# The output stage of a streaming encoder layer: seven half-contraction products for a pair of token tiles in place of eight

## The reference: what is computed

```python
def layer(x, ...):
    proj = jnp.einsum('bld,de->ble', rmsnorm(x, norm_pre), w_in)
    ...                       # three branches: y_gla, y_pool, y_gdn
    merged = gts[:, :, 0] * y_gla + gts[:, :, 1] * y_pool + gts[:, :, 2] * y_gdn
    y = merged.astype(x.dtype) @ w_out          # (2112 x 1024) @ (1024 x 1024)
    x = x + rmsnorm(y, norm_post)
```

## Time and profile before

| | us |
|---|---|
| median of 3 runs | 2485.74 |
| lowest and highest run | 2482.61, 2487.33 |
| profiled execution, first to last instruction | 2480.0 |
| output stage in it: first matmul to last | 2285.5 to 2470.8 |
| end of the last VectorE instruction | 2476.1 |
| PE busy over the span | 2421.5 (98%) |
| VectorE, ScalarE, GpSimd busy over the span | 1104.4, 684.1, 847.1 |

### The profile page before, as it was taken

The page is one execution under the profiler, slowest core; times in us unless marked ns, Lnnn a source line. Parts: engine busy times, 40 slices in busy tenths (PEclk is TensorE's granted clock), DMA queues, the critical chain, the costliest instruction groups (busy, mean ns, idle before and its releaser), DMA issues. The chain is left out here.

```text
span 2480.0 us, 38129 instructions
## 1 busy us (share of the span) xinstructions
PE 2421.5 (98%) x14815; PEld 2263.5 (91%) x14815; DVE 1104.4 (45%) x1867; ACT 684.1 (28%) x1379; POOL 847.1 (34%) x760
## 2 busy tenths in 40 slices
PE   7999999999999999999999999999999979999998
PEld 7989999999999999998999999899998979999886
DVE  6620111223466664006666665666656453224333
ACT  6211111110155531112233223332233243213221
POOL 1212212212111121215556655566555423334222
PEclk9999999999999999999999999999999989999999
DMA  5213512101111122232332343723433174544443
GB/s 168 75 70 113 210 60 78 44 35 49 55 53 52 54 94 79 89 112 78 106 87 80 98 126 89 225 80 99 127 87 86 53 286 167 202 171 133 152 148 101
DMA packets 200892, 264.92 MB, mean 107 GB/s; under 512 B 16224, under 2 KB 176240, under 8 KB 195312
## 3 DMA queue, kind: packets, MB, share of 16 engines
q1 hardware_dynamic: 200816, 263.86, 33.0%
HBM read 164.54 MB, written 99.29 MB: 106 GB/s over the span
## 5 line engine op out<-in xcount | busy, mean ns | idle before, releaser
L393 PE MATMUL dense<-h,w_hi 128*128 128x416 f32 (+1 forms) x1640 | 590.4, 360 | 0.0
L394 PE MATMUL dense<-h,w_hi 128*128 128x416 f32 (+1 forms) x1640 | 582.0, 355 | 0.0
L395 PE MATMUL dense<-h,w_lo 128*128 128x416 f32 (+1 forms) x1640 | 581.4, 354 | 0.0
L188 POOL TENSOR_TENSOR w_hi<-w_raw,zero 128x1024 fp32r<-128x1024 f32 x77 | 148.8, 1933 | 1090.1 <-PE dense L395 795.2
L1443 PE MATMUL gate_bank<-h,w_hi 128*128 128x352 f32 x1632 | 421.7, 340 | 0.2 <-SPq L1301 0.2
L393 PEld LDWEIGHTS dense<-h,w_hi 128*128 128x128 f32 x1640 | 310.1, 189 | 13.5 <-issue 5.7
L394 PEld LDWEIGHTS dense<-h,w_hi 128*128 128x128 f32 x1640 | 308.7, 188 | 11.3 <-issue 4.5
L395 PEld LDWEIGHTS dense<-h,w_lo 128*128 128x128 f32 x1640 | 309.1, 188 | 7.0
L1443 PEld LDWEIGHTS gate_bank<-h,w_hi 128*128 128x128 f32 x1632 | 272.9, 189 | 9.2 <-issue 1.2
L1443 PE MATMUL gate_bank<-h,w_lo 128*128 128x352 f32 x816 | 264.1, 324 | 0.0
L2447 PE MATMUL y<-o_hi,wo_hi 128*128 128x352 f32 x576 | 189.3, 329 | 12.3 <-PEq L107 6.6
(11 more groups left out here) (240 smaller groups left out, 3975.5 us busy)
## 6 DMA issues: line engine op xcount, KB each, us to landing
w_raw<-in_w_in SPq DMA_DIRECT2D x77, 512.0 KB, 5.9
rows_then_inputs<-scratch_feat SPq DMA_DIRECT2D x16, 1856.0 KB, 9.4
scratch_feat<-row_y SPq DMA_DIRECT2D x28, 1056.0 KB, 4.9
gate<-scratch_gates SPq DMA_DIRECT2D x11, 2112.0 KB, 8.6
scratch_gates<-gate_row SPq DMA_DIRECT2D x102, 176.0 KB, 1.8
o_raw<-scratch_branch_out SPq DMA_DIRECT2D x6, 2112.0 KB, 13.5
scratch_h_second<-h SPq DMA_DIRECT2D x2, 4224.0 KB, 19.4
h<-scratch_h_second SPq DMA_DIRECT2D x6, 1408.0 KB, 7.8
```

The source lines that it names most:

```text
L188: nc.gpsimd.tensor_tensor(self.hi[:, p], raw, zeros, ALU.add).then_inc(self.high_ready, 1)
L393: nc.tensor.matmul(out, w_hi[:, p, k], hi.tile(k, t), start=(k == 0), stop=False)
L394: nc.tensor.matmul(out, w_hi[:, p, k], lo.tile(k, t), start=False, stop=False)
L395: mm = nc.tensor.matmul(out, w_lo[:, p, k], hi.tile(k, t), start=False, stop=(k == KD - 1))
```

## The change

The weight and a pair of two token tiles are taken as 2x2 blocks: tokens by contraction halves (A11, A12, A21, A22: 128 tokens by 512) and contraction halves by output halves (B11, B12, B21, B22: 512 by 512). In place of the eight block products the output stage forms seven, of sums and differences of the blocks (the names in the code: `P1` to `P7`; weight sides `B11, T2, T1, T3, B21, B22, T4`), and combines them.

- **PE**: a pair is 7 products of 12 matmuls (4 contraction blocks, 3 parts) in the order P1, P6, P5, P7, P2, P3, P4, in four PSUM banks: P1 and P2 in bank 0, P6 in bank 1, P5 and P3 in bank 2, P7 and P4 in bank 3. The later product of a bank waits until the earlier has been taken out. The code is written out, without a loop.
- **GpSimd**: for each pair the four sums `s1`, `a21` (in place), `s2`, `s4` of 128x512 (`sums`), ahead of the additions of the input row of the pair before (`result`), and one weight difference `T3` of 128x2048.
- **VectorE**: the lower part of each of the seven left operands (`a_low`, 128x512 each), five combinations of a bank with what is there (`taken`), the refined root, and the scaling, which now reads `y_row` in SBUF; for the weight seven lower parts of 128x2048 (`b_low`) and three differences `T1`, `T2`, `T4` of the same size.
- **ScalarE**: seven upper parts of 128x512 a pair and two copies out of bank 0, the squares from `y_row`; seven upper weight parts of 128x2048.
- **SyncE**: one load of `m_raw` for a pair (1 MB) into one of two buffers; the second buffer lies where the first pair's sums and the branch stage's weights are, so that its load waits for all seven weight parts (`b_split`) and six lower parts of pair 0.
- **The sample tile** keeps four half products, of 12 matmuls each, with A of 64 tokens.

The core of the diff:

```diff
+PRODUCTS = 7
+P1, P6, P5, P7, P2, P3, P4 = range(PRODUCTS)
+B_ORDER = (B11, T1, T2, T3, B21, B22, T4)
+PAIRS = CHUNKS // 2
...
+        bank_of = {P1: 0, P2: 0, P6: 1, P5: 2, P3: 2, P7: 3, P4: 3}
+        banks = [y_tok[:, 0], y_tok[:, 1], y[:, 0, 0], y[:, 0, 1]]
+        squares = y[:, 1, 1:3].rearrange("p a b -> p (a b)")
...
@@ sync
+                sp.wait_ge(b_split, PRODUCTS)
                 sp.dma_start(gain[:, :], d["norm_post"].to_broadcast([P, DM])).then_inc(gain_landed, 16)
-                sp.wait_ge(y_ready, LAST * KD + 1)
-                load_x(0, 0)
-                load_x(1, 1)
+                sp.wait_ge(a_split, P4)
+                load_m(1)
+                load_x(0)
+                load_x(1)
+                for i in range(PAIRS):
+                    if i + 2 <= PAIRS:
+                        sp.wait_ge(a_split, PRODUCTS * (i + 1))
+                        load_m(i + 2, 2 * P if i + 2 < PAIRS else NS_)
+                    for t in (2 * i, 2 * i + 1):
+                        store(t)
...
@@ tensor
-                    for half in range(2):
-                        cols = slice(half * 512, half * 512 + 512)
-                        out = tokens_bank(p)[0:n, cols]
-                        for k in range(KD):
+                def product(i, j):
+                    pe.wait_ge(a_split, PRODUCTS * i + j + 1)
+                    if i == 0:
+                        pe.wait_ge(b_split, split_by(j))
...
+                    elif j == P2:
+                        pe.wait_ge(act_taken, 2 * i + 1)
+                    elif j == P3:
+                        pe.wait_ge(dve_taken, 5 * i + 2)
+                    elif j == P4:
+                        pe.wait_ge(dve_taken, 5 * i + 3)
+                    later = j in (P2, P3, P4)
+                    blocks(banks[bank_of[j]], j, j, P, not later, True).then_inc(product_done, 1)
...
@@ vector
+                for i in range(1, PAIRS - 1):
+                    a_low(i + 1, P1)
+                    taken(i, P6)
+                    a_low(i + 1, P6)
+                    taken(i, P5)
+                    a_low(i + 1, P5)
+                    taken(i, P7)
+                    a_low(i + 1, P7)
+                    a_low(i + 1, P2)
+                    taken(i, P3)
+                    a_low(i + 1, P3)
+                    taken(i, P4)
+                    norm(2 * i)
+                    a_low(i + 1, P4)
+                    norm(2 * i + 1)
...
@@ gpsimd
+                def sums(i):
+                    pool.wait_ge(m_landed[i % 2], (i // 2 + 1) * 16)
+                    if i >= 2:
+                        pool.wait_ge(a_split, PRODUCTS * (i - 1) + P3 + 1)
+                    a11, a12, a21, a22 = (raw[:, k:k + 4, t:t + P] for t in (0, P) for k in (0, 4))
+                    tt(s1[:, :, :], a21, a22, ALU.add).then_inc(a_sums, 1)
+                    pool.wait_ge(a_sums, 4 * i + 1)
+                    tt(a21, a11, a21, ALU.subtract).then_inc(a_sums, 1)
+                    tt(s2[:, :, :], s1[:, :, :], a11, ALU.subtract).then_inc(a_sums, 1)
+                    pool.wait_ge(a_sums, 4 * i + 3)
+                    tt(s4[:, :, :], a12, s2[:, :, :], ALU.subtract).then_inc(a_sums, 1)
...
+                for i in range(PAIRS):
+                    if i + 1 < PAIRS:
...
+                        sums(i + 1)
+                    result(2 * i)
+                    result(2 * i + 1)
```

More of the change, by code:

```diff
@@ L2198, in closing_phase @@
[L2198 to L2206, removed]
@@ new lines, in closing_phase @@
+        slot_bytes = 2 * 4 * P * 4
+        slots_at = [raw_at[0] + 2 * ROW, raw_at[1] + 2 * ROW, early.o_at, early.o_at + slot_bytes,
+                    late.end, at, late.ring_at + 5 * ROW]
+        a_hi = [over(f"a_hi{j}", slots_at[j], [P, 4, P], F32R) for j in range(PRODUCTS)]
+        a_lo = [over(f"a_lo{j}", slots_at[j] + slot_bytes // 2, [P, 4, P], F32R) for j in range(PRODUCTS)]
+        assert slots_at[0] + slot_bytes <= late.gate_at + 12 * BT * 4
+        assert slots_at[1] + slot_bytes <= early.o_at and slots_at[3] + slot_bytes <= early.behind_weights
@@ new lines, in closing_phase @@
+        PIECE = 4 * 512 * 4
+        b_at = [(hi_at + q * PIECE, lo_at + q * PIECE) for q in range(5)]
+        gate1_at = late.gate_at + 12 * BT * 4
+        b_at += [(gate1_at, gate1_at + PIECE), (early.slot_at, early.slot_at + PIECE)]
+        under = {B11: 0, T1: 1, T2: 2, T3: 3, B21: 4, B22: 5, T4: 6}
+        b_hi = {q: over(f"b_hi{q}", b_at[n][0], [P, 4, 512], F32R) for q, n in under.items()}
+        b_lo = {q: over(f"b_lo{q}", b_at[n][1], [P, 4, 512], F32R) for q, n in under.items()}
+        t1_raw, t2_raw = (over(f"t_raw{q}", b_at[under[q]][1], [P, 4, 512]) for q in (T1, T2))
@@ L2305, in _ @@
                     if m == 3:
[L2307 to L2312, removed]
+                        sp.dma_start(w_raw[:, KD - 1], d["w_out"][(KD - 1) * P:KD * P, :]).then_inc(w_last_landed, 16)
@@ new lines, in blocks @@
+                def blocks(out, left, q, n, start, stop):
+                    for k in range(4):
+                        matmul(out, a_hi[left][:, k, 0:n], b_hi[q][:, k], start=(start and k == 0), stop=False,
+                               skip_group_check=True)
+                        matmul(out, a_hi[left][:, k, 0:n], b_lo[q][:, k], start=False, stop=False,
+                               skip_group_check=True)
+                        mm = matmul(out, a_lo[left][:, k, 0:n], b_hi[q][:, k], start=False,
+                                    stop=(stop and k == 3), skip_group_check=True)
+                    return mm
@@ new lines, in _ @@
+                a_low(0, P5)
+                a_low(0, P7)
+                taken(0, P6)
+                b_low(B21, b21_raw)
+                for q in range(2):
+                    dve.wait_ge(merged_stored[q], 16 * 4 * TILES_B)
+                nc.vector.memset(eps[:, :], EPS).then_inc(eps_set, 1)
+                taken(0, P5)
+                a_low(0, P2)
+                a_low(0, P3)
+                taken(0, P7)
+                b_low(B22, b22_raw)
+                b_low(T4, t4_raw)
+                a_low(0, P4)
@@ new lines, in _ @@
+                for m in range(KD):
+                    merge(0, m, m % 2, first=True)
+                with pool.Fori(1, LAST) as t:
+                    for m in range(KD):
+                        merge(t, m, m % 2)
+                for m in range(KD):
+                    merge(LAST, m, m % 2)
+                    if m == 4:
+                        pool.wait_ge(w_last_landed, 16)
+                        pool.wait_ge(t_sums, 1)
+                        tt(t3_raw, b22_raw, b12_raw, ALU.subtract).then_inc(t3_ready, 1)
+                    elif m == 5:
+                        sums(0)
```

476 lines of the change are left out of this document (304 added, 172 removed).

## The result

The changed kernel takes 2519.44 us (median of 4 runs, 2517.47 to 2520.89); the kernel before took 2485.42 us on the same chip (2482.61 to 2487.33). The ratio is 1.0139, with a 95% interval of 1.0124 to 1.0153: 34 us slower. The profiled execution of the changed kernel has a span of 2517.1 us, 37.1 over the one before. The forecast was 2510, with rival 1 at 2521. Of the 37.1 us between the two profiled executions some 3 belong to the executions themselves: the runs' medians lie 34 us apart, and TensorE began the closing phase, ahead of which no instruction differs, at 1996.5 us in the one before and at 1999.5 in this one.

A forecast was written before the change was run, and what follows sets the result against it. The prediction took PE, busy 98% of the span, as the bound. Terms 24.2 + 2.2 + 0.8 - 2.7 = +24.5 us on 2485.7 gave 2510, own range 2503 to 2517, 8 in 10 within 2496 to 2522.

The forecast's parts named there:

- rival 1: Steady part: the clock falls with every pair's wait for bank 2, 5 x 2.2 = +11 us, 2521; chance 16%.
- three waits over 5 us: Sign of being right: three PE waits over 5 us within 2283 to 2350, granted clock under 1 behind them.
- start, until pair 2 begins: Weight split and pair 1: start ends 24.2 us late, plus 2.2 for the clock behind the 8.4 us stall.
- pairs 2 to 6: Steady output stage: a pair takes 21.92 us for 21.76 before, +0.16 five times, +0.8 us.
- last pair: Last pair of the output stage: no sums behind it, so 19.04 us, a gain of 2.7 us.
- Walk A: Weight at the start: VectorE and GpSimd exclude each other link by link, 39.5 us, all seven parts there at 2313.5.
- Walk B: Pair 1: load landed at 2321.9, then links of 25.85 us; P3 starts at 2347.8 after 8.4 us waiting.
- Walk C: Steady pair: 16.48 us from P4's end until P3 may start; PE there at 13.6, so waits 2.9 us.
- Rival 2: VectorE and GpSimd: exclusion costs less, scaling from SBUF not taking part or sums nearer 1.15; about -7 us, 2503; 14%.
- Rival 3: VectorE's and GpSimd's 512-column instructions run side by side: pair 19.2 to 19.4 us, total 2483, up to 2464; 10%.
- Rival 4: PE's queue: the change does not issue fewer matmuls; given no chance.
- the hoped 21.8 us: PE in the output stage: 96 matmuls fewer over eight pairs, 21.8 us less if PE never waits.

The follow-up runs named there:

- experiment 1: Changed kernel with P5 and P7 taken out of their banks before the lower part of the next pair's P6 in VectorE's queue: 2487.88 us, ratio 1.0012.
- experiment 7: Changed kernel with GpSimd's difference T3 formed on 8 of its 512 columns: 2516.26 us, ratio 1.0125.
- Experiment 3: Changed kernel with pair 1's load asked for after six of pair 0's lower parts, ahead of the last weight parts and the gain: 2508.57 us, ratio 1.0098.
- experiment 2: Changed kernel with idle matmuls in front of P3, 30 in pair 1 and 12 in pairs 2 to 6: 2508.92 us, ratio 1.0097.
- experiment 5: Changed kernel with the edits of experiment 1 and Experiment 3 together: 2479.89 us, ratio 0.9981.
- experiment 6: experiment 5 with ScalarE copying P2 before rounding the next pair's parts, and the start of pair 1 arranged alike: 2480.48 us, ratio 0.9987.

## Why the prediction was right, and where its size was off

The direction was right, by the mechanism it named: the kernel is slower because VectorE and GpSimd exclude each other, and the walk through both holds a bank. What it did not see is that the order in VectorE's queue alone puts this walk in front of the bank (experiment 1). The forecast of 2510 was 9.4 us short, outside its own range of 2503 to 2517; the number was that of rival 1, 2521. By its own signs too: it called a pair of over 24 us the sign of rival 1, and the pair took 24.05; of the three waits over 5 us that it named two came (6.34 and 6.91), and one was 4.75. Placed on the traces, from start to start of matmuls:

| piece | predicted, us | measured, us |
|---|---|---|
| ahead of the walks | 0 | +2.1 (gating of block 4 at 2270.45 for 2268.31) |
| start, until pair 2 begins (2329.0 before) | 24.2 + 2.2 = +26.4 | 2356.88, +27.9, so +25.7 without the first row |
| pairs 2 to 6 | 5 x 0.16 = +0.8 | 5 x (24.05 - 21.76) = +11.5 |
| last pair | -2.7 | 19.60 - 21.76 = -2.2 |
| the end, behind the last pair | 0 | 16.38 - 16.52 = -0.1 |

The first row is no effect of the change as far as the runs tell: in the executions of the changed kernel and the experiments the closing phase began anywhere from 1996.6 to 2002.2, though they differ in nothing ahead of it, and the one of the kernel before, at 1996.5, was an early one. Without this row, the others sum to +34.9 for the forecast's +24.5.

**Walk A** (the weight parts): the gain, with pair 1's load right behind it, was asked for at 2313.75, for 2313.7 forecast. The waits inside came as 1.56, 4.75, none and 0.78 us for 3.2, 5.9, 2.1 and 2.2; these misses lie inside the walk. Part of this agreement is luck: the walk began 1.0 us later than forecast (T2 at 2275.01 for 2274.03) and was shorter by as much, and experiment 7 shows that not every link of the sum is on the path by its full length.

**Walk B** (pair 1): GpSimd's first sum began at 2322.7 (2321.9 forecast), P3 started at 2348.49 (2347.8), after 6.91 us of waiting (8.4), and P3 with P4 took 8.39 us where 5.44 + 2.2 was allowed. Experiment 3 moved its first link and all the rest went with it.

**Walk C** (the steady pair): from the end of P4 at 2357.04 to P3 at 2373.72 it is 16.7 us; 16.48 was forecast, and the wait 2.7 for 2.9. It is right in sum and wrong in one link: the one-column steps were priced at 0.70 everywhere, and the second group of them waits for GpSimd's `x_again` (2.19 us in place of 0.16). This did not lengthen the walk, since the second scaling was held back by the same addition in the forecast; the wait came one instruction sooner.

**The step that was mis-sized is the steady pair**, in the words of the prediction: "with P3 and P4 the pair is 21.92 us for 21.76 before: +0.16, five times". P3 and P4 were put at 5.44 us, and took 7.4 (24.05 less 16.7). Of the 1.9 us over, 1.5 are the clock: in experiment 2 they take 5.70 us from the start of P3 to that of the next P1, for 7.22. The rest is 24 matmuls at 0.2333 for 0.2267, 0.16; the end of the last matmul, 0.16 behind the start of the next, which a sum by starts leaves out; and 0.1 at the first matmul behind a wait. The prediction had the mechanism, as rival 1 (5 x 2.2 = +11, given 16%), and had charged the clock to the waits over 5 us alone, because rows 9 show a fall behind a wait of that length. The traces show it behind 2.7 us too. The size came from a row at one length, and nothing in the rows said that a shorter wait would be free.

**The rivals.** Rival 2 (scaling does not take part) is not borne out: the three-operand form takes part even on one column, and GpSimd's sums take 1.26 to 1.31 us in the steady pairs, not 1.15. Rival 3 (side by side) is refuted by VectorE's lower part of P6, which takes 1.17 us where 0.68 is usual and is over 0.55 us behind the end of GpSimd's sum:

```profile
2419.27 1.27 POOL L2842 TENSOR_TENSOR sum_then<-m_raw,sum_then 128x512 f32<-128x512 f32 x1
2419.92 1.17 DVE L2663 TENSOR_TENSOR a_lo<-sum_then,a_hi 128x512 fp32r<-128x512 f32 x1 [6.28 <-ACT a_hi L2413]
```

Its figure for the steady part, 19.2 to 19.4, nevertheless came near by another way: in experiment 1 the pair takes 19.59 us with all exclusions in place, because they no longer stand in front of the bank. Rival 4 is out: the page counts 96 matmuls fewer.

**Where the hoped 21.8 us are**, in experiment 5: the pace of the matmuls takes 8 x 0.55 = 4.4 back; TensorE's waits, 1.57 + 4.74 + 0.32 + 0.30 + 0.54 + 0.16 + 0.99 + 1.10 = 9.7; the clock behind the wait of 4.74 slows seven matmuls by about 0.2 us each, 1.4. That leaves 6.3 of the 21.8, where 5.0 was measured; the last 1.3 us were not placed.

## What to carry to other kernels

When TensorE is full and its work is cut, walk the other engines' queues through one period, and look at what stands between the last read of a bank and its release: here it was two independent lower parts ahead of an addition that TensorE waited for, and moving them was worth 31.6 us. Price each wait that is left with its clock: a wait of 2.7 us cost 1.6 us again. Idle matmuls buy that back only if TensorE's own work sets what comes next.

## What the runs showed of the hardware

- A wait of 2.66 to 2.68 us was enough for the granted clock to fall to 0.50, in all five steady pairs, and the fall came only after the work had resumed: matmuls 0.23 us apart until 1.0 us behind the restart at 2397.77, then 0.43, until 2402.43 (timeline of PE):

```profile
2398.54 0.40 PE L2572 MATMUL y<-b_hi,a_hi 128*128 128x512 f32 x1
2398.78 0.56 PE L2574 MATMUL y<-b_lo,a_hi 128*128 128x512 f32 x1
2399.14 0.63 PE L2576 MATMUL y<-b_hi,a_lo 128*128 128x512 f32 x1
2399.57 0.63 PE L2572 MATMUL y<-b_hi,a_hi 128*128 128x512 f32 x1
```

  The fall does not always come that late: in experiment 7, behind waits of the same 2.66 to 2.68 us, the first matmul was already a slow one in each steady pair (0.76 us for 0.47). Behind the waits of 1.53 and 1.73 us in experiment 6 the clock stayed at 1.00.

- The exclusion of VectorE and GpSimd goes by instruction and not by size. A three-operand step of one column in SBUF waited 2.19 us for GpSimd's 1024-column addition, and took 0.16 without it; the step ahead of it has one operand in SBUF and did not wait, in the middle of the same addition:

```profile
2407.99 2.73 POOL L2848 TENSOR_TENSOR x_again<-normed,x_again 128x1024 f32<-128x1024 f32 x1 [11.52 <-DVE normed L2708]
...
2408.37 0.15 DVE L2692 TENSOR_SCALAR stat<-stat 128x1 f32<-128x1 f32 x1
2408.55 2.19 DVE L2696 SCALAR_TENSOR_TENSOR stat<-stat 128x1 f32<-128x1 f32 x1
```

  The Trainium skill ("SBUF — State Buffer", section "Who interferes with whom") has the rule for a VectorE operation with two SBUF inputs against a GpSimd operation that reads SBUF; the traces agree (2.19 us for 0.16), and add that one column is enough. GpSimd's side is the same: 32 numbers of a row took 2.36 us behind VectorE's T2.
- Matmuls of 512 columns with the same left and right shapes came 0.2267 us apart in one program and 0.2333 in the other, at a granted clock of 1.00 and with no wait. It does not hang on the order within three, nor on the product or its bank, nor on the program as a whole (idle matmuls in the second program have 389 ns again). The cause was not found.
